# Padded keys, column-wise joints and reordered small steps in a fused four-layer forward pass on one core

## What is computed

```python
def second_block(x, ...):
    for l in range(DEPTH):                                     # DEPTH = 2
        h = x @ w_in[l] + b_in[l]
        lru_x, lru_gate, q, kc_raw, vc_raw, ks_, vs_, kw_, vw_, gts = jnp.split(h, offsets, axis=-1)
        y_lru = _rg_lru(lru_x, lru_gate, ...)                  # conv, gates, scan over tokens, * gelu(gate)
        kc = _compress(kv(kc_raw), ...); vc = _compress(kv(vc_raw), ...)
        y_nsa = _nsa(q, kc, vc, kv(ks_), kv(vs_), kv(kw_), kv(vw_), gts)
        mix = jnp.concatenate([_rms_norm(y_lru, ...), _rms_norm(y_nsa, ...)], axis=-1) @ w_out[l]
        x = _layer_norm(ALPHA * x + mix, ...)
        x = _layer_norm(ALPHA * x + _peer(x, ...), ...)
```

## Time and profile before

| | us |
|---|---|
| median of 3 runs (2850.66 to 2853.05) | 2851.88 |
| the profiled execution, its own time | 2847.72 |
| its span, first to last instruction | 2845.9 |
| PE busy (share of the span) | 2758.4 (97%) |
| PEld busy | 2425.3 (85%) |
| DVE busy | 2207.0 (78%) |
| ACT busy | 1601.2 (56%) |
| POOL busy | 86.7 (3%) |
| mean granted TensorE clock, share of full speed | 0.992 |

### The profile page before, as it was taken

The page is one execution under the profiler, slowest core; times in us unless marked ns, Lnnn a source line. Parts: engine busy times, 40 slices in busy tenths (PEclk is TensorE's granted clock), DMA queues, the critical chain, the costliest instruction groups (busy, mean ns, idle before and its releaser), DMA issues.

```text
span 2845.9 us, 45138 instructions
## 1 busy us (share of the span) xinstructions
PE 2758.4 (97%) x16972; PEld 2425.3 (85%) x16972; DVE 2207.0 (78%) x3851; ACT 1601.2 (56%) x2771; POOL 86.7 (3%) x150
## 2 busy tenths in 40 slices
PE   8988999999999999999999999999999999999998
PEld 5776887977888879999998888887899999988886
DVE  4766888886655568999887888865789988788787
ACT  3433554344554644678895554545457789755553
POOL 1000111000002000000000000020000000000000
PEclk9999999999999999999999999999999999999999
DMA  8433776764556235666668777752466666687775
GB/s 297 151 113 132 270 266 252 239 236 156 190 186 225 94 120 182 213 212 203 199 196 265 242 242 240 234 196 71 142 197 219 206 204 194 214 262 242 241 242 164
DMA packets 211288, 579.69 MB, mean 204 GB/s; under 512 B 24096, under 2 KB 87872, under 8 KB 210048
## 3 DMA queue, kind: packets, MB, share of 16 engines
q1 hardware_dynamic: 161568, 491.00, 53.3%
q0 software_dynamic: 13792, 53.28, 5.6%
q10 hardware_dynamic: 35712, 32.52, 3.3%
HBM read 541.05 MB, written 35.65 MB: 203 GB/s over the span
## 4 chain that ended last, share of the span: by engine, by line
PE 84%; DVE 11%; ACT 3%; issue 1%; DMA 1%; ACTq 0%; DVEq 0%; POOLq 0%
PE psum L758 83%; DVE gmem L2160 3%; DVE wr L2160 2%; ACT gmem L1549 1%; DVE gmem L2163 1%; DVE xmem L2163 1%; ACT crf L1549 1%; DVE xr L2160 1%; PE psum L839 0%; DMA raw<-in_hyb_qkv 0%; DVE oh_r L2163 0%; ACT wr L1549 0%; DVE xmem L2160 0%; DVE small L2939 0%; DVE gmem L3053 0%
## 5 line engine op out<-in xcount | busy, mean ns | idle before, releaser
L2160 DVE TENSOR_TENSOR wr<-raw,wr 128x1024 fp32r<-128x1024 f32 (+1 forms) x814 | 995.0, 1224 | 407.3 <-ACT wr L1549 402.2
L758 PE MATMUL psum<-xr,wr 128*128 128x256 f32 (+1 forms) x9760 | 1290.6, 292 | 17.3 <-DVE xr L2160 9.1
L758 PEld LDWEIGHTS psum<-xr,wr 128*128 128x128 f32 x9760 | 1234.4, 192 | 62.7 <-DVE xr L2160 14.5
L1549 ACT ACTIVATE wr<-raw 128x1024 fp32r<-128x1024 f32 x808 | 848.0, 1050 | 274.3 <-PE psum L758 247.9
L758 PE MATMUL psum<-wr,cr 128*128 128x512 f32 x3072 | 697.4, 389 | 5.0 <-DVE cr L2160 5.0
L758 PEld LDWEIGHTS psum<-wr,cr 128*128 128x128 f32 x3072 | 576.5, 188 | 125.5 <-ACT cr L1549 3.3
L1549 ACT ACTIVATE cr<-xmem 128x256 fp32r<-128x256 f32 x256 | 107.2, 419 | 338.9 <-PE psum L758 336.8
L1549 ACT ACTIVATE gmem<-psum 128x512 f32<-128x512 f32 (+2 forms) x303 | 169.0, 570 | 208.2 <-PE psum L758 182.7
L758 PE MATMUL psum<-wr,xr 128*128 128x512 f32 (+1 forms) x960 | 234.7, 398 | 4.8 <-DVE xr L2160 1.7
L758 PEld LDWEIGHTS psum<-wr,xr 128*128 128x128 f32 x960 | 175.2, 192 | 48.0 <-issue 6.0
L2163 DVE SCALAR_TENSOR_TENSOR oh_r<-cst,keep,keep_r 128x256 fp32r<-128x256 f32 x512 | 213.0, 477 | 0.0
(11 more groups left out here) (173 smaller groups left out, 1526.2 us busy)
## 6 DMA issues: line engine op xcount, KB each, us to landing
raw<-in_uv SPq DMA_DIRECT2D x512, 512.0 KB, 4.8
raw<-in_ffn_in SPq DMA_DIRECT2D x88, 512.0 KB, 3.6
gs<-xmem ACTq DMA_DIRECT2D x248, 128.0 KB, 3.7
xmem<-gs SPq DMA_DIRECT2D x248, 128.0 KB, 4.4
gmem<-in_ada_w POOLq DMA_DIRECT2D x56, 512.0 KB, 5.0
raw<-in_ffn_out SPq DMA_DIRECT2D x44, 512.0 KB, 3.8
raw<-in_ada_w SPq DMA_DIRECT2D x40, 512.0 KB, 4.1
raw<-in_ret_a SPq DMA_DIRECT2D x32, 512.0 KB, 4.4
```

The lines of the kernel that those rows point to most:

```text
L758: ins = pe.matmul(o, a, b, start=first and i == 0, stop=final and i == len(pairs) - 1, skip_group_check=skip)
L1549: return act.activation(o, a, func, **k)
L2160: return dve.tensor_tensor(o, a, b, op)
```

## The change

1. Keys. `kv` keeps only the two columns of the compressed branch. The keys of the other branches go to `kz`, a zero-padded copy for each key head, 128 partitions with the other head's half zero. ACT writes each key column in two instructions of 64 partitions, POOL zeroes the rest with two more memsets in each mixer. `att_scores` multiplies 128 rows; TensorE waits once for the zeros.
2. Joints. `out_last` waits for both units first and then finishes one bank after the other, with a signal for each; DVE waits for each bank rather than each half.
3. Compressed weights. `cmp_weights` runs on DVE after the maximum of st 1, not ahead of that of st 0.
4. Compressed turn. `cmp_turn` uses bank 7 in place of 6.
5. Recurrence. The last subtraction of `lru_y` becomes a step `lru_lo` one st later, behind `att_exp` of st 7.
6. Last row unit. `mix_out_a(l, 1, 1)`, at st 10, comes after `att_values(l, 9)`, not ahead of it.
7. `layer_norm` with a split after it issues `busy(7, 7)` in place of `busy(7, 5)`.

```diff
@@ mixer2
-            if st in (6, 7, 9, 10):
+            if st in (6, 7, 9):
                 s["mix_out_a"](l, st // 9, (st - 6) % 3)
...
             if st > 0:
                 s["att_values"](l, st - 1)
+            if st == 10:
+                s["mix_out_a"](l, 1, 1)
...
+            if st == 4:
+                s["lru_lo"](l)
@@ tensor_program
         def out_last(b, c_of, ks, sig):
-            pair = {}
-            for a in range(2):
-                for k in ks:
-                    if k not in pair:
-                        pair[k] = next_unit()
-                    j, hi, lo = pair[k]
-                    for n in range(2):
-                        e = slice(512 * n, 512 * n + 512)
+            held = [next_unit() for _ in ks]
+            for a in range(2):
+                for n in range(2):
+                    e = slice(512 * n, 512 * n + 512)
+                    for k, (j, hi, lo) in zip(ks, held):
                         ch, cl = c_of(k)
                         ins = mm3(bank(b + 2 * a + n), [...], False, k == ks[1], True)
-                    if a:
-                        ins.then_inc(*W.pe.up(j))
-                    elif k == ks[1]:
-                        ins.then_inc(*X.pe.up(("half", sig)))
+                        if (a, n) == (1, 1):
+                            ins.then_inc(*W.pe.up(j))
+                    if (a, n) != (1, 1):
+                        ins.then_inc(*X.pe.up(("half", sig, a, n)))
...
         def cmp_turn(l):
-            claim(6)
+            claim(7)
...
         def att_scores(l, st):
+            pe.wait_ge(*zeroed[l, "kz"])
-                pr, m = head(h0 + i)
-                ins = mm(o[:, i, :], [(nqT[pr, m, quarter(a)], kv[pr, 1 + br, 0:w_])], False, i == nh - 1, True)
+                hh = h0 + i
+                ins = mm(o[:, i, :], [(nqT[:, hh % 4, quarter(a)], kz[:, hh // 4, br, 0:w_])], False, i == nh - 1, True)
...
         def layer_norm(tag, src, g, b_, split):
             if split:
-                busy(7, 5)
+                busy(7, 7)
@@ scalar_program, mix_col
+                elif c in (12, 15):
+                    f(kv[:, c // 15, :], src, AF.Identity, bias=bias).then_inc(*X.act.up(("col", l, j)))
                 else:
-                    f(kv[:, c - 12, :], src, AF.Identity, bias=bias).then_inc(*X.act.up(("col", l, j)))
+                    for g in range(2):
+                        r = slice(64 * g, 64 * g + 64)
+                        f(kz[r, g, c - 13, :], src[r], AF.Identity,
+                          bias=bias[r]).then_inc(*X.act.up(("col", l, j) if g else None))
@@ vector_program
             for a in range(2):
-                dve.wait_ge(*(done() if a else X.pe["half", name]))
                 for n in range(2):
+                    dve.wait_ge(*(done() if (a, n) == (1, 1) else X.pe["half", name, a, n]))
...
         def lru_y(l):
             tt(gl, gl, xc, ALU.mult).then_inc(*L.dve.up(("y", l)))
+
+        def lru_lo(l):
             dve.wait_ge(*L.act["hi", l])
-            own(L)
+            dve.wait_ge(*L.dve["y", l])
             tt(xr[:, 1, 0:4, :], gl, xr[:, 0, 0:4, :].bitcast(F32), ALU.subtract).then_inc(*L.dve.up(("lo", l)))
...
         def att_scores(l, st):
-            if st == 0:
-                cmp_weights(l)
+            pass
 
         def att_exp(l, st):
...
+            if st == 1:
+                cmp_weights(l)
@@ pool_program
+            for g in range(2):
+                pool.wait_ge(*zeroed.now)
+                pool.memset(kz[64 - 64 * g:128 - 64 * g, g], 0.0).then_inc(*zeroed.up((l, "kz") if g else None))
```

More of the change, by code:

```diff
@@ L2927, in layer_norm @@
             for a in range(2):
-                dve.wait_ge(*(done() if a else X.pe["half", tag]))
                 for i in range(2):
+                    dve.wait_ge(*(done() if (a, i) == (1, 1) else X.pe["half", tag, a, i]))
                     v = src[:, a, 512 * i:512 * i + 512]
@@ L3264, in pool_program @@
             pool.wait_ge(*zeroed[l, "hv"])
-            for i, (src, pos) in enumerate(((0, "posk"), (3, "posv"))):
+            for i, (src, pos) in enumerate(((0, "posk"), (1, "posv"))):
                 for g in range(2):
```

14 lines of the change are left out of this document (7 added, 7 removed).

## The result

The changed kernel takes 2824.84 us (median of 4, 2822.76 to 2825.85); the kernel before, run beside it, 2851.76 (2850.66 to 2853.05). The ratio is 0.9904, 95% interval 0.9888 to 0.9920: 26.9 us faster. The profiled execution took 2824.49 us.

The account below looks back on a forecast made before the run. TensorE, busy 97% of the span, was taken as the bound. Mixers 7.85 and 8.25, residuals 1.4, expert layers' ends 1.3 and clock -1.6 summed to 17.2 us: 2851.9 - 17.2 = 2834.7 us, range 2827 to 2844.

Parts of the forecast that it names:

- the charge: Both mixers: half a clock fall of 1.6 us charged in each for new waits, -1.6 us in the sum.
- The first rival: Attention of both mixers: no clock falls, 5.4 us more gained, 2829.3 us; chance 0.18.
- the middle stretches: Each mixer, up to the last scores: 3.3 us gained, 1.16 plus 7 banks x 0.31; clock loss of 1.6 left.
- Padded keys: Score banks: 128 rows save 0.31 us a bank, 7.4 us of PE time over 24 banks, 0 to 9.6.
- the second and third rivals: Score banks: second, padding gives nothing, 2842.1 us, chance 0.10; third, padded loads not hidden, 2866.8 us, chance 0.02.
- Weights later, turn in another bank: Mixers up to att_values(0): 5.1 and 5.5 us gained, a new 1.7 us wait there, set by DVE.
- Recurrence's remainder: At att_values(4): the 1.16 us wait for DVE's bank 7 scaling goes, gaining 1.16 us in each mixer.
- Last row unit: Before nsa_turn(0): a 1.1 us wait is removed but PE only waits later; worth 0.
- Joints: Layer outputs: residuals gain 1.4 us, expert layers' ends 1.3; mixers' outputs lose 0.55 each, with PE waiting 1.35.
- The expert layers' ends: Ends of both expert layers: one DVE addition moves into idle time, gaining 0.64 us each, 1.3 in all.
- The residuals: Four residual joints: DVE is free 0.34 us earlier, gaining 0.35 us each, 1.4 in all.
- The base: Whole kernel: the median is 4.2 us above the profiled execution, so the forecast starts from 2851.9 us.

Follow-up runs that it names:

- f0: The changed kernel, unedited, run again beside later runs: 2824.18 us.
- f3: The changed kernel with out_last's first half unit by unit and lru_scan moved behind the first attention step: 2819.04 us, ratio to before 0.9884.
- f1: The changed kernel with out_last's first half again unit by unit, the second bank by bank: 2820.65 us.
- e1: The kernel before with padded keys (item 1) alone: 2841.12 us.
- e2: The kernel before with items 3 to 6 alone, no padding and no joints: 2837.62 us.
- h4: The kernel before with item 5 alone, the recurrence's last subtraction one st later: 2844.15 us.
- e0: The kernel before, unchanged, run beside itself: 2850.82 us, ratio 1.0003.
- e3: The kernel before with items 2 and 7 alone (joints, seven idle matmuls for five): 2847.73 us, ratio 0.9990.
- g1: The kernel before with four unused fp32 matmuls added ahead of the first att_turn's wait in each mixer: 2848.98 us, ratio 0.9995.
- h1: The changed kernel with item 3 undone, compressed weights again ahead of the maximum of st 0: 2825.00 us.

## Why the prediction was wrong, step by step

**What the clock costs.** Two executions of one kernel give a price: f0 has a fall of 3.4 us in mixer 2 (1950.5) that the changed kernel's first profile lacks, and is 140.58 - 138.95 = 1.63 us longer there, 0.48 us for each us at half clock. The fall at 890 us is cheaper: f3 has it and f1 has not, and from the retention output to the first bank they take 258.52 and 257.13 us, 1.4 us for 3.4. Where PE also waits for DVE it is cheaper still. In the stretch from the last bank to idle the two falls cost 0.65 and 0.85 us (27.27 to 27.30 without one in e1, e2 and h4), and in the norms 0.6 and 0.7 (11.93 to 11.95 without one in e1, e2 and h4).

**The clock is the step that failed.** The forecast treated only the fall at the first turns as something to win back, charged 0.8 us in each mixer for new falls and left every other fall as it was. Compared behind the first part, the profiles differ by 26.2 us, 9.0 more than the sum's 17.2. Of these, 1.6 are the charge, for falls that did not come; 1.6 the fall at 1972 us, which had no term and went; 2.8 the falls at 1017, 1037, 1993 and 2013 us, which went too; and 1.4 the one at 890 us. That is 7.4 of 9.0. The rest is 0.7 in the residuals and 0.9 spread over the stretches. In the whole gain the clock's share is about half: 17 us less of low time at the first turns, at 0.40 to 0.48 an estimated 7 to 8 us, with the 5.8 just named. The first rival, full clock everywhere, had the mechanism, but it priced in only the middle stretches and one layer norm, so it ended at 2829.3, with a chance of 0.18.

**What was right.** Where the falls were as the sum assumed, it holds. From the first bank to `att_values(0)` the mixers gained 5.4 and 5.8 us (5.1 and 5.5 forecast), both ending on DVE as said; in the middle stretch of mixer 1, where a fall stood in both kernels, 3.5 (3.3).

**Padded keys.** Two banks in a row lie 950.80 - 949.71 = 1.09 us apart (the first two 0.99), against 1.16 forecast. From turn to turn, with what comes before and behind the bank, 2.77 us became 2.38 ((982.92 - 977.38) / 2 before, (975.76 - 971.01) / 2 after), and with a bank of four heads 2.80 became 2.41. So a bank saves 0.39 us, 24 banks 9.4 of PE's own time, not 7.4. The sum itself holds only 7 banks a mixer, 4.3 us, since DVE sets the start of `att_values(0)`; the second and third rivals took 7.4 off it, which it did not contain. Without a fall the changed kernel shows 6.0 us for the padding (above). The failed number is 0.24 us for one instruction of 256 columns on 128 rows, read off a group that held a short wait; it is 0.22. The upper bound, 0.40 a bank, held. The rival "padding gives nothing" and the slower one, loads no longer hidden, are refuted: padded matmuls start 0.22 us apart beside weight loads of 0.19 us. By the rule of the Trainium skill ("TensorE: Matmul & The Clock Gate", section "Packing small matmuls") each load would have added its time; no trace here bears that out for fp32 operands of 128 rows.

**Weights later, turn in another bank.** Right in what is next, a wait ahead of `att_values(0)`, released by DVE, 1.36 us long, and right in what the pair does to the kernel before: 4.8 and 5.2 us in that stretch by e2, which has no padding. What the prediction does not say is that the two stand in for each other and for the padding. Undone singly in the changed kernel they cost 0.7 us and nothing in each mixer: either order leaves DVE's chain about where it is.

**Recurrence's remainder.** 1.16 us in each mixer was right for the wait in the kernel before. In the changed kernel the same wait would be 2.15 us, and the item is worth 4.8 us by the parts at equal low time, 5.8 by the medians.

**Last row unit.** The waits were right (0.3 us between the orders); the 3.1 us by the medians go with the clock.

**Joints.** The expert layers' ends gave 0.67 us each (0.64), one in the norm at the start of mixer 2 and one behind the last matmul. The wait ahead of the mixers' last matmuls is 1.34 us (1.35), and the norm behind gives about 0.75 back (0.8). So the 1.33 and 1.41 us of the expert layers' parts are this 0.75 and the two falls that went. The residuals, 0.35 us each in the sum, made their own norms 0.59, 1.00, 0.59 and 0.59 us shorter. What reaches the parts is less, since PE can wait for the second unit ahead of the joint (0.22 us at the first feed-forward output): 0.07, 0.89 and, without the fall at 890 us, 1.15 us, 2.1 in all against 1.4. What the hybrid output's joint costs ahead of its norm can't be told under the falls of the first part.

**The base.** Carrying the 4.2 us between profile and median to the changed kernel was right for the medians. e0 shows what it is: falls of the clock in the first part, more or fewer from one execution to the next.

**Still open** is what makes the clock fall at a given place. At the first turn these combinations were run:

| keys | wait at the first turn, us | low time there, mixers 1 and 2, us |
|---|---|---|
| 64 rows (before) | 1.14, none | 6.8, 10.2 |
| 64 rows (e3) | none, none | 10.2, 10.2 |
| 64 rows (h4) | 1.14, 1.14 | 6.8, 3.4 |
| 64 rows (g1, e2) | none, none | 0, 0 |
| 128 rows (e1) | 2.14, 2.14 | 3.4, 3.4 |
| 128 rows (h1) | 2.13, 2.13 | 0, 0 |

Neither 64-row keys nor the wait is enough by itself, and neither is needed: e3 and mixer 2 of before have the longest falls with no wait, beginning 2.2 to 2.5 us behind the first bank, and e1 has one with 128 rows. The same code has a fall in one execution and none in another (f0 and the changed kernel in mixer 2). No run shows what decides.

## What to carry to other kernels

Give the time at half clock a term of its own: add it up over a whole stage, layer norms included, and treat all of it as recoverable, in the range at least, when an edit thins out waits there. Here a us at half clock cost 0.4 to 0.5 us where PE ran without a pause and 0.2 where it also waited for DVE. Find the engine that ends last behind a set of waits before crediting any of them: three waits of PE here hung on one DVE chain, so undoing one item moved the wait and cost 0.7 us in a mixer where its own wait read 2.1, while two items together were worth 3.2. Take the same stages' lengths from two executions of the unchanged kernel before comparing with a third; here 3.7 us of difference was in a part of one and the same kernel.

## What the runs showed of the hardware

Passing between 64 and 128 rows costs about 0.1 us at each of four places of a bank. PE one by one, kernel before (start, length; the counts end with the stretch that was asked for), then the changed kernel:

```profile
977.74 0.48 PE L758 MATMUL psum<-al_r 128*128 128x512 f32 x1
...
978.15 0.48 PE L758 MATMUL psum<-gmem 64*128 64x256 f32 x1
...
978.47 0.81 PE L758 MATMUL psum<-gmem 64*128 64x256 f32 x3
...
978.90 0.63 PE L758 MATMUL psum<-gmem 64*128 64x256 f32 x2
979.21 0.44 PE L758 MATMUL psum<-gmem 128*128 128x64 f32 x2
```

```profile
971.37 0.47 PE L762 MATMUL psum<-al_r 128*128 128x512 f32 x1
...
971.68 0.38 PE L762 MATMUL psum<-gmem 128*128 128x256 f32 x1
...
971.90 0.60 PE L762 MATMUL psum<-gmem 128*128 128x256 f32 x2
972.11 0.59 PE L762 MATMUL psum<-gmem 128*128 128x256 f32 x2
```

With 64 rows the first key matmul starts 0.41 us after the bias and the second 0.32 after the first; between the inner two it is 0.22 (978.47 to 978.90, two steps), and from the last into the next 128-row matmul 0.31; the one after that follows 0.16 later. With 128 rows the numbers are 0.31, then 0.22 throughout, and 0.06 for the last. Together that is the 0.39 us of a bank. Half of the multiplied rows are zeros, and it is faster all the same.
